# Sparse mixer of a two-block transformer stack: order of the row maxima's sums, the compressed exponentials and the first score tiles

## What is computed

```python
def nsa_mixer(x, w_in, cmp_pos, cmp_w1, cmp_b1, cmp_w2, w_out):
    proj = x @ w_in
    ...
    k_cmp = compress(kv[0, 0], cmp_pos[0], cmp_w1[0], cmp_b1[0], cmp_w2[0])
    v_cmp = compress(kv[0, 1], cmp_pos[1], cmp_w1[1], cmp_b1[1], cmp_w2[1])
    ...
        s = jnp.einsum('bgrqd,bgcd->bgrqc', qc, k_cmp, preferred_element_type=f32)
        s = s - sl * (tf[:, None] - cmp_center[None, :])
        p_cmp = masked_softmax(s, m_c) * m_c
        o_cmp = jnp.einsum('bgrqc,bgcd->bgrqd', p_cmp.astype(dt), v_cmp)
        ...
        p = masked_softmax(s, dist >= 0)
        o_sel = jnp.einsum('bgrqk,bgqkd->bgrqd', p.astype(dt), vg)
        ...
        p = masked_softmax(s, m_w)
        o_win = jnp.einsum('bgrqk,bgkd->bgrqd', p.astype(dt), vw)
        o = gc[0] * o_cmp + gc[1] * o_sel + gc[2] * o_win
    return o @ w_out
```

## Time and profile before

| | |
|---|---|
| median of 3 runs | 3112.69 us (3112.5 to 3112.69) |
| profiled execution, own time | 3111.14 us |
| its span, first to last instruction | 3109.3 us |
| PE busy | 3022.3 us (97%) |
| DVE / ACT / POOL busy | 1868.5 (60%) / 1252.9 (40%) / 304.2 (10%) us |
| mean granted TensorE clock | 0.993 |

### The profile page before, as it was taken

One profiled execution on the slowest core, in us unless ns is written; L12 is line 12 of the kernel. 1 busy time (PEld: TensorE's weight loads), 2 busy tenths in 40 slices (PEclk: granted clock), 3 DMA queues, 4 the chain that ended last, 5 costly groups with the idle time before them and its releaser, 6 DMA issues.

```text
span 3109.3 us, 37010 instructions
## 1 busy us (share of the span) xinstructions
PE 3022.3 (97%) x14782; PEld 2393.4 (77%) x14782; DVE 1868.5 (60%) x2959; ACT 1252.9 (40%) x2004; POOL 304.2 (10%) x222
## 2 busy tenths in 40 slices
PE   8999999999999999999999999999999999999998
PEld 4878887877888677767777777888887866788887
DVE  5877775245435677784545786666436675566632
ACT  3344524135432344534454474322225656322222
POOL 0012200001100002202210030000003210000000
PEclk9999999999999999999999999999999999999999
DMA  5222132320012322222113233233332310233332
GB/s 209 68 75 75 48 102 97 110 87 28 21 35 78 105 82 82 72 85 70 45 55 92 74 97 96 93 95 92 98 95 85 116 38 1 89 95 94 92 97 70
DMA packets 78733, 251.50 MB, mean 81 GB/s; under 512 B 9122, under 2 KB 11170, under 8 KB 78562
## 3 DMA queue, kind: packets, MB, share of 16 engines
q1 hardware_dynamic: 72672, 227.91, 23.6%
q0 software_dynamic: 5024, 18.09, 1.9%
q10 hardware_dynamic: 864, 3.15, 0.3%
HBM read 247.01 MB, written 2.10 MB: 80 GB/s over the span
## 4 chain that ended last, share of the span: by engine, by line
PE 47%; ACT 3%; DVE 3%; issue 1%; DMA 0%; DVEq 0%; ACTq 0%
PE PS L1168 32%; PE PS L1806 5%; PE PS L2851 3%; PE PS L2946 1%; PE PS L1930 1%; ACT WH L1117 0%; PE PS L2911 0%; PE PS L2927 0%; PE PS L2873 0%; ACT PS L2994 0%; PE PS L2912 0%; PE PS L2928 0%; ACT PTN L3008 0%; PE PS L2579 0%; PE PS L1910 0%
## 5 line engine op out<-in xcount | busy, mean ns | idle before, releaser
L1127 DVE TENSOR_TENSOR WL<-RAW,WH 128x1024 fp32r<-128x1024 f32 (+3 forms) x374 | 424.7, 1136 | 476.0 <-ACT WH L1117 474.9
L1117 ACT ACTIVATE WH<-RAW 128x1024 fp32r<-128x1024 f32 (+3 forms) x397 | 384.6, 972 | 437.7 <-PE PS L1168 332.5
L1806 PE MATMUL PS<-Hh,WH 128*128 128x512 f32 x1376 | 524.8, 381 | 14.4 <-DVE WL L1127 7.7
L1806 PE MATMUL PS<-Hl,WH 128*128 128x512 f32 x1376 | 487.3, 354 | 0.0
L1806 PE MATMUL PS<-Hh,WL 128*128 128x512 f32 x1376 | 485.6, 353 | 0.0
L1806 PEld LDWEIGHTS PS<-Hh,WH 128*128 128x128 f32 x1376 | 259.9, 189 | 74.2 <-issue 21.6
L1168 PE MATMUL PS<-XH,WH 128*128 128x512 f32 x768 | 305.0, 397 | 0.0
L1168 PE MATMUL PS<-XH,WL 128*128 128x512 f32 x768 | 303.4, 395 | 0.0
L1168 PE MATMUL PS<-XL,WH 128*128 128x512 f32 x768 | 303.4, 395 | 0.0
L1806 PEld LDWEIGHTS PS<-Hl,WH 128*128 128x128 f32 x1376 | 260.1, 189 | 47.4 <-issue 10.1
L1806 PEld LDWEIGHTS PS<-Hh,WL 128*128 128x128 f32 x1376 | 260.3, 189 | 40.4
(11 more groups left out here) (403 smaller groups left out, 5712.4 us busy)
## 6 DMA issues: line engine op xcount, KB each, us to landing
RAW<-in_w_in SPq DMA_DIRECT2D x124, 512.0 KB, 3.6
RAW<-in_ffn_in SPq DMA_DIRECT2D x96, 512.0 KB, 3.6
RAW<-in_ffn_out SPq DMA_DIRECT2D x48, 512.0 KB, 3.5
RAW<-in_w_ada SPq DMA_DIRECT2D x32, 384.0 KB, 3.4
RAW<-in_nsa_in SPq DMA_DIRECT2D x21, 512.0 KB, 3.3
RAW<-in_lru_in SPq DMA_DIRECT2D x20, 512.0 KB, 3.6
MW<-in_w_ada SPq DMA_DIRECT2D x32, 256.0 KB, 9.7
BS<-in_bs POOLq DMA_DIRECT2D x16, 512.0 KB, 3.9
```

Source lines behind the costliest of these rows:

```text
L1117: act.activation(WH[half[j]][:, 0:n], RAW[j % NRAW][:, 0:n], ACT.Copy).then_inc(*did("act_whi", ("whi", j)))
L1127: dve.tensor_tensor(WL[half[j]][:, 0:n], RAW[j % NRAW][:, 0:n], WH[half[j]][:, 0:n].bitcast(F32), ALU.subtract).then_inc(*did("dve_wlo", ( ...
L1806: mm = pe.matmul(ps[:, c:c + w_], wt[:, 128 * k:128 * k + 128], x[:, a:a + w_], start=(k == 0 and q == 0), stop=(k == n - 1 and q == 2))
```

## The change

Four things in the order of the list, and nothing in what is computed:

1. In the step (17 + `qt`, 1) of the projections, the last maximum's `sum` is issued ahead of `cexp` (new helper `settle`), and the units `low` of that step too.
2. `c2out` 1 goes from step (17, 0) to (17, 4).
3. The transition has no maxima any more: seven of them, 83 to 89, go to the scores.
4. `MOST[1]` goes from 0.8 to 1.0, one maximum per score tile.

```diff
-MOST = (0.65, 0.8)
+MOST = (0.65, 1.0)
...
+    def settle(self):
+
+        i = self.nmax
+        if self.settled < i:
+            self.unit("sum", i - 1)
+            if i % 32 == 0:
+                self.unit("raise", i // 32 - 1)
+            if i == 32:
+                self.unit("k2", 0)
+        self.settled = i
+
     def most(self, n):
 
         for _ in range(n):
             i = self.nmax
-            if i > 0:
-                self.unit("sum", i - 1)
-                if i % 32 == 0:
-                    self.unit("raise", i // 32 - 1)
-                if i == 32:
-                    self.unit("k2", 0)
+            self.settle()
...
-              (12, 4): [("hid", 0)], (13, 0): [("c2", 0)], (13, 4): [("c2out", 0)], (16, 2): [("hid", 1)], (16, 6): [("c2", 1)], (17, 0): [("c2out", 1)]}
+              (12, 4): [("hid", 0)], (13, 0): [("c2", 0)], (13, 4): [("c2out", 0)], (16, 2): [("hid", 1)], (16, 6): [("c2", 1)], (17, 4): [("c2out", 1)]}
...
+        for qt in range(4):
+            w = (17 + qt, 1)
+            rest = [u for u in at[w] if u[0] != "cexp"]
+            lows = [u for u in rest if u[0] == "low"]
+            at[w] = [("settle",)] + lows + [("cexp", qt)] + [u for u in rest if u not in lows]
...
         for w in sorted(at):
             for u in at[w]:
                 self.unit(*u)
-            self.most(1)
         for qt in range(4):
             self.unit("rows", 0, qt)
-            self.most(1)
```

More of the change, by code:

```diff
@@ L762, in nsa @@
         self.pt = Ring(list(range(8)))
-        self.norder, self.nmax, self.ninner = [], 0, []
+        self.norder, self.nmax, self.settled, self.ninner = [], 0, 0, []
         self.nsa_projections()
@@ L888, in nsa_projections @@
                 for u in at.pop((i, k), []):
-                    self.unit(*u)
+                    if u[0] == "settle":
+                        self.settle()
+                    else:
+                        self.unit(*u)
                 if (i, k) >= (4, 4) and (i, k) not in ((12, 5), (12, 6), (16, 3), (16, 4)):
```

## The result

| | before | change |
|---|---|---|
| median of 6 runs each | 3110.36 us (3106.21 to 3112.69) | 3120.32 us (3118.56 to 3124.45) |
| profiled execution, its span | 3111.14, 3109.3 us | 3119.19, 3117.4 us |
| busy PE, DVE, ACT | 3022.3, 1868.5, 1252.9 us | 3023.3, 1868.0, 1252.6 us |
| mean granted clock | 0.993 | 0.994 |

The change takes 1.0032 times as long, with an interval of 1.0022 to 1.0042: slower by more than 0.2%. The forecast was no measurable difference, with a range up to 3117.5. (The forecast of 3112.2 stood on a median of 3112.69 from the three runs known then; with six runs the median of before is 3110.36, which makes the miss larger.) A repeat in a later group of runs gave 1.0033. The engines' totals moved by a few tenths of a microsecond up to 1.0; the 8.1 us more of the span are waiting and slowed time.

The account below looks back on a forecast made before the run. PE, 97% busy, was taken as the bound, with only its idle or slowed time to win and DVE its next limit. Terms -0.8 and +0.3 gave -0.5 us: 3112.2 us against the median 3112.69, range 3107.5 to 3117.5.

Parts of the forecast that it names:

- Part 1: Projections: PE's 3.3 us stall goes, shorter waits for DVE replace it; DVE ends 0.5 us behind its old time.
- slack of 0.9: Third chain in the projections: PE had 0.9 us to spare, so a DVE 0.5 us late would not delay it.
- The 16-column product: Second chain on DVE: it would again be held by POOL's subtraction, near 2.4 us; 2.2 us kept in the forecast.
- `raise` and POOL: Projections on DVE: `raise`, due at 2487.7, may be held by POOL's first subtraction, making DVE 0.7 us later; middle taken.
- Rival A: Second chain in the projections: PE's wait there brings a second slow stretch; +4.2 us, giving 3116.4; chance 0.23.
- the sentence against A: Block 15 in the projections: the wait of 2.0 us may bring the slow level earlier, where PE has time to spare.
- Part 2: Transition: 2.5 us gained, less 1.7 for running slow again; -0.8 us together with the projections; first score tile about 2530.3.
- its slow stretch: Around the first score tile: PE let run slow again as before, costing 1.7 us.
- 2.0 us for seven maxima: Scores: PE owes the seven moved maxima, 2176 columns twice at 0.24 us per 512, 2.0 us.
- Part 3: Scores: seven more sums raise ACT from 57.8 of 77.2 us to some 61.4 of 79; +0.3 us taken.
- The bound of +3.6: Scores: the cost if all of ACT's added load were exposed, +3.6 us.
- Rival C: Scores: ACT becomes the bound, above about 95% in the first 45 tiles, on top of Rival A; +7.0, 3119.7; chance 0.05.

Follow-up runs that it names:

- p1: Against the change: seven maxima back in the transition, 0.8 maxima a tile, projections as changed; 3113.88 us, 1.0006 of the kernel before.
- q2: Against the change: the last maximum's sum issued on ACT ahead of every score tile; 3113.48 us, 1.0007 of the kernel before.
- q1: Against the change: in every fourth score tile the maximum goes behind the value products; 3113.04 us, 1.0008 of the kernel before.
- p3: Against the change: 0.9 maxima a score tile instead of 1.0; 3119.65 us, 1.0021 of the kernel before.
- r2: Against p1: sum and `low` ahead of the exponential for the first query tile alone, values copied as before; 3110.55 us, 0.9995 of the kernel before.
- s1: Against r3: the last maximum's sum issued ahead of every score tile; 3106.39 us, 0.9982 of the kernel before.
- s2: Against q2: two of the seven moved maxima put back in the transition; 3115.85 us, 1.0011 of the kernel before.
- p2: Against the kernel before: transition without maxima and 1.0 maxima a tile, projections unchanged; 3119.32 us, 1.0020.
- r3: Against r2: the values' copy moved to step (17, 4), as in the change; 3109.92 us, 0.9993 of the kernel before.
- q3: Against the kernel before: in every fourth score tile the maximum goes behind the value products; 3109.24 us, 0.9996.
- p4: Against the kernel before: 1.0 maxima a tile, the transition's maxima kept; 3114.39 us, 1.0009.
- q4: Against p4: in every fourth score tile the maximum goes behind the value products; 3115.69 us, 1.0012 of the kernel before.
- r1: Against the kernel before: the last maximum's sum issued on ACT ahead of each score tile's exponential; 3107.94 us, 0.9988.
- s3: Against p4: the last maximum's sum issued ahead of every score tile; 3110.12 us, 0.9992 of the kernel before.

## Why the prediction was wrong

- **Part 1, right in its places.** Forecast: waits of 0.8, 2.0 or more and up to 3.5, second transposes at 2502.4. Measured: 0.74, 2.21 and 2.65, and 2502.44. The 16-column product met POOL again (2.37 us). The third transposes came at 2512.76 with a wait of 0.16: DVE's chain ended 0.56 us later than before (0.5 forecast) and PE came 0.4 earlier, which together used up its slack of 0.9.
- **`raise` and POOL.** I took the middle between 0 and 0.7. The row shows 0.57 us instead of 0.19: held until POOL's subtraction ended, 2485.97 + 2.37 = 2488.34. The Trainium skill, "SBUF — State Buffer", section "Who interferes with whom", lets a VectorE instruction with two SBUF inputs block while a GpSimd instruction reads SBUF. This trace agrees, at a price of 0.4 us.
- **Rival A did not occur in the change, and did in two other traces of the same order.** From 2484 to 2503 the change lost 19.0 x 0.09 = 1.7 us where before had lost 5.1. They lie behind the wait of 2.21 us at block 15, as the sentence against A had it: from about 2491.3 to 2494.6 TensorE is at 1.2 GHz. After the wait of 2.65 us the clock is 1.00 to 2524.9. In p1, whose projections are ordered as in the change, the second wait was 1.44, and behind it:

```profile
2503.00:2525.50 22.50, 22.37 (x112) 18.93 (x110) 18.56 (x45) 9.16 (x24) 1.05 (x2) 0.86 0.14 42
```

  22.5 x 0.14 = 3.2 us. q2, again of the same order, had 0.83 in this stretch, behind a wait of 2.47. The other five traces of that order, the change's among them, had waits of 2.56 to 2.67 and stayed at 1.00. The length of one wait, on which I let A turn, does not decide it, and neither does the order of the instructions; that the change's own trace was free of A is partly luck. The rule that stood behind A (the Trainium skill, "TensorE: Matmul & The Clock Gate", section "HAM oscillation — how this bites in real kernels"), that an idle gap takes the clock down and each gap is paid anew, is borne out by these runs in part only. The gap of 3.30 us was followed by the lower level in all seven traces that have it, at a clock of 0.64 or 0.73 over 2484 to 2503; the shorter ones of 1.44 in p1 and 2.47 in q2 were too, and those of 2.56 to 2.67 in the other five were not.
- **Part 2, right in the gain, short in the clock.** The first tile starts at 2529.97; forecast 2530.3. But its slow stretch was taken over at before's 1.7 us and measured 8 x 0.35 = 2.8 from 2530 to 2538, with 5.1 x 0.12 = 0.6 ahead of it, where PE is mostly idle. One mis-sized term, of 1.1 to 1.7 us. The prediction's 2.0 us for seven maxima is right at its own point of comparison, the start of before's third tile, ahead of which the seventh stands; in the transition itself there are six.
- **Part 3 is the step that failed.** Its term was +0.3, between 0 and +3.6, and it came from ACT's busy share: 57.8 of 77.2 us, to rise to 61.4 of 79. The tiles instead cost 11.3 us more. Without the 1.8 that PE owed and the 1.9 of the slow stretch, both of which belong to part 2, 7.6 us stand where the term had 0.3: 5.9 of PE's idle time, 4.6 of them in waits for sums, and 1.7 left over. The bound of +3.6 held all of ACT's added work exposed, and was no bound, since what is exposed is not the sum's own 0.5 us but the queue ahead of it: a tile's exponential and the mask that it waits for. Two facts were there to be read before: that maxima have three banks, and that with one per tile a burst holds four (with 0.8 it holds three, and four in every fifth burst). I priced a ring by the load of the engine that frees it.
- **Rival C had the time, 3119.7, by another mechanism, and that is luck.** It wanted ACT above 95% on top of A; ACT was at 69%, and A did not occur. The case that came, a ring freed through a queue that isn't full, was missing from the list.

What stays open: why the first microseconds of the scores run slow and by how much (0.64 in q1, p3 and the repeat, 0.65 in the change, 0.74 in r2, 0.75 in s1, 0.79 in s2 and p2, 0.84 in q2, 0.86 in r3 and q3, 0.88 or 0.89 in p1, p4, q4, r1, s3 and before); why nine tenths leave the stage as long as one per tile; and 1.7 us of the 11.3, for which there is only the estimate above. A fourth bank for maxima was not tried, nor were tiles without masks.

## What to carry to other kernels

Where a producer hands out banks of a ring and another engine frees them, count how many it issues in one burst and compare with the ring. If there are as many or more, price the wait by what stands ahead of the releasing instruction in its engine's queue, waits included, and not by the engine's busy share. Work that frees a bank belongs ahead of work that may wait for a third engine: one unit moved ahead of each tile's exponential was worth 0.12% in the kernel before and twice that in the change. An edit that removes one stall is worth trying at that place alone: here, made at the first of four places, it shortened the projections by 2 us in three traces, and made at all four it shortened them in none of seven. Neither could be told from no change by the median alone.

## What the runs showed of the hardware

- **DVE held by POOL, again at the same length.** A product of 16 columns that lasts 0.23 us alone took 2.37 while POOL subtracted for 2.34, in the change as in the kernel before, and an operation of 32 columns took 0.57 instead of 0.19. Small operations on DVE can be the dearest ones there.
- **The clock can be at its lower level with PE never idle.** The first 8 us of the change's scores, cut in two:

```profile
2530.00:2534.00 4.00, 4.00 (x12) 3.23 (x12) 3.45 (x8) 1.52 (x4) 1.81 (x1) 0.50 0.01 2
2534.00:2538.00 4.00, 4.00 (x26) 2.84 (x25) 1.87 (x6) 3.18 (x10) 0.00 (x0) 0.80 0.00 0
```

  PE is busy throughout, and at 0.50, 1.2 GHz, for four of them; what came ahead were 5.1 us with PE at 2.23. Missing filler in the transition is not the whole reason, since s1 and r2, whose transitions kept their maxima, had 0.75 and 0.74 there. In the kernel before the same is seen for longer: behind the stall of 3.30 us, from 2488 to 2497 us, PE is busy for all of the nine microseconds and the granted clock is 0.50.
- **One order, two clocks.** The same order of the projections gave 1.00 from the second transposes on in five traces and 0.86 or 0.83 in two, worth 3.2 and 4.2 us. One profiled execution does not tell the clock of a stretch that follows a wait.
